# Block 1's gate branch: 512-column products into two banks a slab, the bank pairs in another order, the last GELU behind two tanh groups

## The chip, the cores and the metric

The kernel runs on one core of one Trainium2 chip. The metric is the device time of one execution in microseconds (us), the median of several runs; less is better.

## What is computed

A sequence of 256 positions with 1024 features passes through two transformer-like blocks. The change lies in the first block, in the branch that gates the recurrent unit. Cut to that part, the reference is:

```python
h = rmsnorm(x, norm1_g[l])
u = jnp.einsum('bsd,de->bse', h, w_in[l])
x_rnn, g_rnn, q, k, v, g_br = jnp.split(u, list(cuts), axis=-1)
xa = causal_dwconv(x_rnn, conv_w[l], conv_b[l])
ya = rg_lru(xa, w_r[l], b_r[l], w_i[l], b_i[l], lru_lambda[l]) * jax.nn.gelu(g_rnn)
q = rmsnorm(q.reshape(bsz, s, N_HEADS, HEAD_DIM), q_norm_g[l]).transpose(0, 2, 1, 3)
...
```

`g_rnn` has 1024 features. It is a product of `h` (256 positions, 1024 features) with 1024 columns of `w_in`, and `gelu(g_rnn)` is multiplied into the output of the recurrent unit. Everything is float32 at the interface.

## The kernel before, in words

Each float32 operand of a product is split into a high part (rounded to the format that TensorE multiplies) and a low part (what the rounding left). A product then is three products: high weight by high activation, high weight by low activation, low weight by high activation.

**Slabs.** All weights come in slabs of 128 partitions by 2048 numbers, numbered in the order of use (`s` in the code), through a ring of three buffers. For each slab SyncE loads `raw`, ScalarE (ACT) makes `whi` (line 547), VectorE (DVE) makes `wlo` from `raw` and `whi` (line 1012) and counts `lo_ready`, and TensorE waits for that count before the slab's first matmul. The calls `pre(s)` stand in the programs of ACT and of DVE between their other work, in an order written by hand; each engine runs its program strictly in that order, and semaphores tie the engines together. I call ACT's half of slab s "high part s" and DVE's half "low part s".

**The slabs around the change.** Slabs 0 to 3 are the columns of `x_rnn` (the first two come with the input). Slabs 4 to 7 (`S_G` on) are the gate branch `g_rnn`, 256 features each, and the change is about them. Slab 8 (`S_RI`) holds the small block matrices of the recurrent unit's two gates: eight groups of six matmuls, each group into one PSUM bank, banks 0 to 3 taken twice; ACT empties each by two tanh instructions (line 710), and groups 4 to 7 wait until the bank's earlier group was emptied. Slabs 9 on (`S_Q`) are halves of strips of q, k and v.

**A gate slab before.** `feature_tiles` makes it: for each of 8 slices k and each of 2 tiles of 128 features it calls `three` (lines 1632, 1635, 1636), three matmuls of 256 columns into one half of one PSUM bank, 48 matmuls a slab. DVE multiplies the bank by the position's norm factor `rstd_bc` straight into `gg` (`normed`, line 1056), and ACT takes the GELU of it in place (line 702). Beside that DVE runs the three further taps of the convolution (`taps`, line 1153), ACT makes the high part of `xa` (line 680) and GpSimd (POOL) its low part (line 1568). Behind the last gate slab and low part 9, DVE runs a chain of 23 tiny instructions for softplus (lines 1180 to 1191, "the softplus chain") and only then low part 10.

**PSUM.** The eight banks of 512 columns are also seen as four pairs, `pp[0]` to `pp[3]`. Bank 7, half of `pp[3]`, holds for a while the norm factors turned into a column (`PSB`), which DVE copies into `rstd_half` and `rstd_sq` (lines 1173, 1174) and then counts `rstd2_ready`.

**The other form of product.** `feature_pairs` (lines 1674 and 1676) is in use already for the w_out slabs and the feed-forward layers. High and low activation lie side by side in `ahilo`, so one matmul of 512 columns does both products with the high weight, into a whole bank, and one of 256 columns does the third. A slab then fills two banks, and the half of each bank that holds high weight by low activation must be added to the other. In the feed-forward layers ACT copies that half out (`cross`, line 817), DVE adds the other half to it (line 1335) and then multiplies by `rstd_bc` (lines 1348 and 1368).

The lines of DVE's program around the change:

```python
taps(S_G - 1)
for s in range(S_G, S_RI):
    i = s - S_G
    normed(GROUP_OF[(s, 0)], gg[:, 2 * i:2 * i + 2, :])
    if i == 0:
        e.wait_ge(row_T, 1)
        ...
    if s == S_G + 1:
        pre(s + 3)
pre(S_RI + 1)
```

Of the kernel before, what the change touches and what calls it, by code (L numbers as in the profile page):

```python
# [17 lines left out]
SEQ = 256  # L18
# [140 lines left out]
    return groups  # L159


GROUPS = group_plan()
GROUP_OF = {(s, i): g for g, (s, i, _) in enumerate(GROUPS)}


def bank_plan():


    banks, last, before = [], {}, []
    for g, (s, i, _) in enumerate(GROUPS):  # L170
        if half_strip(s) is not None:
            banks.append(i)
            before.append(None if half_strip(s) else last[i])
            last[i] = g
            continue
        if strip_of(s) is not None:
            b = None
        elif s < S_RI:
            b = s % 4
        elif s == S_RI:  # L180
            b = i % 4
        elif s in (S2_OSWA + 1, S2_OMLA + 1):
            b = 2 + i
        elif out_slab(s) is not None:
            b = ((3, 1) if s < FFN1 else (1, 3))[out_slab(s) % 2]
        elif s in (S2_UQ + 1, S2_UKV):
            b = (3, 2)[i] if s < S2_UKV else (0, 1, 3, 2)[i]
        else:
            b = g % 2
        before.append(last.get(b))  # L190
        banks.append(b)
        last[b] = g
    return banks, before
# [56 lines left out]
def program(nc, t):  # L250
    f32, f32r = mybir.dt.float32, mybir.dt.float32r
    ALU, ACT, AX = mybir.AluOpType, mybir.ActivationFunctionType, mybir.AxisListType.X
    with ExitStack() as ctx:
# [3 lines left out]
        def sem(name):  # L257
            return ctx.enter_context(nc.semaphore(name))
# [103 lines left out]
        def out_pair(s):  # L362

            return pp[((1, 0) if s < FFN1 else (0, 1))[out_slab(s) % 2]]
# [44 lines left out]
            "h_hi", "h_lo", "sq_ready", "ssum", "rms_root", "rstd_ready", "rms_root2", "rstd2_ready"))  # L409
        sq_fold = sem("sq_fold")  # L410
        xa_ready, xa_hi, xa_lo = sem("xa_ready"), sem("xa_hi"), sem("xa_lo")
        g_ready = sem("g_ready")
        t_ready, sqt_ready, ya_ready, ya_hi, ya_lo = (
            sem(n) for n in ("t_ready", "sqt_ready", "ya_ready", "ya_hi", "ya_lo"))
        head_sq, head_sums = sem("head_squares"), sem("head_sums")
# [117 lines left out]
        def _(e):  # L533
# [15 lines left out]
            def pre(s):  # L549
                if s < SLABS:  # L550
                    hi(s % RING, raw_value(s), used_value(s - RING) if s >= RING else None)

            def free_bank(ins):
                ins.then_inc(bank_free["act"], 1)
# [122 lines left out]
            def xa_parts(s):  # L677

                e.wait_ge(xa_ready, s + 1)
                e.activation(pairs[1][0][:, 2 * s:2 * s + 2, :], xa[:, 2 * s:2 * s + 2, :], ACT.Copy).then_inc(xa_hi, 1)  # L680

            for s in range(S_XR, S_G):
# [10 lines left out]
                if s < S_XR + 2:  # L693
                    pre(s + 5)
            pre(S_RI)
            xa_parts(S_G - 1)
            for s in range(S_G, S_RI):
                if s == S_G + 2:
                    pre(s + 3)
                i = s - S_G  # L700
                e.wait_ge(bank_free["dve"], s + 1)
                e.activation(gg[:, 2 * i:2 * i + 2, :], gg[:, 2 * i:2 * i + 2, :], ACT.Gelu_apprx_tanh).then_inc(g_ready, 1)

            for i in range(8):
                g = GROUP_OF[(S_RI, i)]
                e.wait_ge(group_done, g + 1)
                for m in range(2):
                    blk = 2 * (i % 4) + m
                    dst = (T0 if i < 4 else T1)[:, blk, :]
                    ins = e.activation(dst, ps[BANK[g]][:, SEQ * m:SEQ * m + SEQ], ACT.Tanh, scale=0.5,  # L710
                                       bias=halfb[:, 8 * (i // 4) + blk:8 * (i // 4) + blk + 1])
                free_bank(ins)
                if i == 3:
                    pre(S_RI + 2)
            e.wait_ge(bank_free["act"], 8)
# [285 lines left out]
        def _(e):  # L1001
# [13 lines left out]
            def pre(s):  # L1015
                if s < SLABS:
                    lo(s, s % RING)
# [142 lines left out]
            for s in range(S_XR, S_G):  # L1160
                if s >= 2:
                    e.wait_ge(xa_ready, s - 1)
                normed(GROUP_OF[(s, 0)], xrp[:, s % 2, :, KW - 1:])
                if s:
                    taps(s - 1)
                pre(s + 4)
            taps(S_G - 1)
            for s in range(S_G, S_RI):
                i = s - S_G
                normed(GROUP_OF[(s, 0)], gg[:, 2 * i:2 * i + 2, :])  # L1170
                if i == 0:
                    e.wait_ge(row_T, 1)
                    e.tensor_scalar(rstd_half[:, :], PSB[:, 0:2], 0.5, None, ALU.mult)
                    e.tensor_copy(rstd_sq[:, :], PSB[:, 0:2]).then_inc(rstd2_ready, 1)
                if s == S_G + 1:
                    pre(s + 3)
            pre(S_RI + 1)
# [451 lines left out]
        def _(e):  # L1629
# [8 lines left out]
            def bank_ready(g):  # L1638

                s, i = GROUPS[g][:2]  # L1640
                if s in (S2_GA, S2_GA + 1):
                    e.wait_ge(bank_free["dve"], emptied(GROUP_OF[(FFN1, 2 * STEPS - 1)])[1])
                elif s == S2_UQ + 1:
                    e.wait_ge(*((aTe, pair(3)) if i else (cq_lo, 5)))
                elif s == S2_OSWA + 1:
                    e.wait_ge(rope_q_act, 2)
                    e.wait_ge(rope_q_dve, 2)
                elif BEFORE[g] is not None:
                    who, n = emptied(BEFORE[g])
                    e.wait_ge(bank_free[who], n)  # L1650
# [263 lines left out]
            def slab(s, act, layout="feature", ready=always, hook=None):  # L1914

                if s > 2:
                    e.wait_ge(lo_ready, s + 1)
                slot = s % RING
                kind = PLAN[s][1]
                if half_strip(s) is not None:  # L1920
                    half_strips(s, act, ready, hook)
                    return
                if kind == "strip":
                    strips(s, act, lambda k: (hook() if hook and k % 4 == 2 else None, ready(k)))
                    return
                n = sum(1 for x in GROUPS if x[0] == s)
                for i in range(n):
                    g = GROUP_OF[(s, i)]
                    bank_ready(g)
                    out = ps[BANK[g]]  # L1930

                    def at(k, i=i):

                        if (i, k) == (0, 0):
                            pairs_first(s)
                        if (i, k) == ((0, 4) if n == 1 else (n // 2, 0)):
                            pairs_second(s)
                        if (s, i, k) == (S2_OMLA + 1, 1, 0):
                            merge_turn(2)
                        if hook and (i, k) == (0, 4):  # L1940
                            hook()
                        if s == 2 and k % 4 == 0:
                            e.wait_ge(*((lo_ready, 3) if k else (first_lo, KD - 1)))
                        ready(k)

                    if kind == "blocks":
                        for m in range(2):
                            blk = 2 * (i % 4) + m
                            c = 1024 * (i // 4) + P * blk
                            ins = three(out[:, SEQ * m:SEQ * m + SEQ], tuple(w[slot][:, c:c + P] for w in (whi, wlo)),  # L1950
                                        (act[0][:, blk, :], act[1][:, blk, :]), m == 0, True)
                    elif out_slab(s) is not None:
                        ins = feature_pairs(out_pair(s), slot, at, ACT0)
                    elif layout == "feature" and kind == "cols":
                        ins = feature_tiles(out, slot, KD, WIDE, act, [(0, 0), (P, SEQ)], ready=at)
                    elif S2_OSWA <= s < S2_OUT:
                        ins = positions(out, slot, 4, 512, act, slice(0, 512), [(i, 0)],
                                        k0=4 if s >= S2_OMLA else 0, ready=at)
                    elif kind == "nope" or (kind == "kv" and i < 2):
                        ins = feature_tiles(out, slot, 3 if kind == "nope" else 2, HEADS * NOPE, act,  # L1960
                                            [(2 * P * i, 0), (2 * P * i + P, SEQ)], k0=0 if kind == "nope" else 3,
                                            ready=at)
                    elif kind == "rope":
                        ins = positions(out, slot, 3, HEADS * ROPE, act, slice(0, HEADS * ROPE), [(i, 0)], ready=at)
                    else:
                        ins = positions(out, slot, 2, HEADS * VD, act, slice(0, HEADS * VD), [(i - 2, 0)], k0=3,
                                        ready=at, w0=2)
                    ins.then_inc(group_done, 1)
# [263 lines left out]
```

## Time and profile before

| what | value |
|---|---|
| median of 3 runs | 791.01 us (790.78 to 791.04) |
| the profiled execution's own time | 790.45 us |
| its span from first to last instruction | 788.7 us |
| TensorE busy | 781.8 us, 99% |
| VectorE busy | 592.8 us, 75% |
| ScalarE busy | 453.0 us, 57% |
| GpSimd busy | 44.3 us, 6% |
| granted TensorE clock | 0.999 of full speed |

The profile lists for each engine its instructions by start and duration, in us from the start of the span. Two neighbours on one engine overlap a little, so I take the distance of two starts as what an instruction costs its engine. A row's bracket says how long the engine sat idle before it, and what ended that. A matmul's end is modelled; its start is what to read. A row may merge neighbours of one kind, and then gives their number.

### The profile page before, as it was taken

The page shows a single profiled execution, that of the slowest core. Times are in us where ns is not written, and L with a number is a line of the kernel's source. Part 1 is how long each engine was busy: PE and PEld are TensorE (multiplying, and loading weights), DVE is VectorE, ACT ScalarE, POOL GpSimd, SP SyncE. Part 2 cuts the span into 40 slices and gives each one's busy share as a digit, 9 for nine tenths or more (in the row PEclk, how much of TensorE's full clock was granted, in tenths as well). Part 3 has the DMA queues.
Part 4 walks back from the last instruction along what each step waited for, and adds up shares of the span by engine and source line. Part 5 has one row for each costly group of instructions (what it writes and reads, how often), then busy time and mean ns, then how long its engine had stood idle before and what let it go on. Part 6 is the DMA issues. An engine that isn't in the chain of part 4 may idle for free.

```text
span 788.7 us, 11267 instructions
## 1 busy us (share of the span) xinstructions
PE 781.8 (99%) x4246; PEld 669.7 (85%) x4246; DVE 592.8 (75%) x731; ACT 453.0 (57%) x595; POOL 44.3 (6%) x63
## 2 busy tenths in 40 slices
PE   9999999999999999999999999999999999999997
PEld 9998888888888888888888897888788888888886
DVE  6986897666578998778887867787789666666664
ACT  7679765666345654444445758766455545454444
POOL 0220331000000000000000031120000000000000
PEclk9999999999999999999999999999999999999999
DMA  8745555443545455555554452444435545454521
GB/s 331 244 175 193 198 180 214 156 160 128 192 160 207 152 206 184 188 200 197 183 189 160 157 222 89 153 180 160 159 138 212 214 160 208 166 210 167 206 106 53
DMA packets 22100, 141.08 MB, mean 179 GB/s; under 512 B 3410, under 2 KB 3762, under 8 KB 6066
## 3 DMA queue, kind: packets, MB, share of 16 engines
q1 hardware_dynamic: 21682, 140.13, 49.2%
q10 hardware_dynamic: 384, 0.49, 0.2%
q8 instruction: 22, 0.36, 0.2%
q14 instruction: 12, 0.10, 0.0%
HBM read 139.33 MB, written 1.05 MB: 178 GB/s over the span
## 4 chain that ended last, share of the span: by engine, by line
PE 97%; ACT 1%; issue 1%; DVE 1%; ACTq 0%
PE pp L1674 24%; PE pp L1632 18%; PE pp L1636 18%; PE pp L1635 18%; PE pp L1676 12%; PE pp L1818 1%; PE pp L1843 1%; PE pp L1830 1%; PE pp L1994 1%; PE pp L1986 0%; PE pp L1983 0%; PE pp L1979 0%; PE pp L1884 0%; PE pp L1728 0%; PE pp L1756 0%
## 5 line engine op out<-in xcount | busy, mean ns | idle before, releaser
L1012 DVE TENSOR_TENSOR wlo<-raw,whi 128x2048 fp32r<-128x2048 f32 x129 | 296.3, 2298 | 82.5 <-ACT whi L547 81.9
L547 ACT ACTIVATE whi<-raw 128x2048 fp32r<-128x2048 f32 x129 | 246.2, 1910 | 96.9 <-PE pp L1636 81.1
L1674 PE MATMUL pp<-ahilo,whi 128*128 128x512 f32 x832 | 261.9, 396 | 0.1
L1676 PEld LDWEIGHTS pp<-ahilo,wlo 128*128 128x128 f32 x832 | 156.3, 188 | 36.7
L1676 PE MATMUL pp<-ahilo,wlo 128*128 128x256 f32 x832 | 163.5, 278 | 0.0
L1632 PE MATMUL pp<-whi,ahilo 128*128 128x512 f32 (+1 forms) x336 | 133.8, 398 | 0.2 <-ACT first L778 0.2
L1636 PE MATMUL pp<-whi,ahilo 128*128 128x512 f32 (+1 forms) x336 | 130.5, 388 | 0.0
L1635 PE MATMUL pp<-wlo,ahilo 128*128 128x512 f32 (+1 forms) x336 | 130.4, 388 | 0.0
L1674 PEld LDWEIGHTS pp<-ahilo,whi 128*128 128x128 f32 x832 | 128.3, 189 | 2.0 <-DVE wlo L1012 0.3
L817 ACT ACTIVATE qk<-pp 128x512 f32<-128x512 f32 x44 | 26.3, 599 | 118.6 <-PE pp L1676 118.6
L1632 PE MATMUL pp<-whi,ahi 128*128 128x512 f32 (+1 forms) x218 | 85.0, 390 | 0.0
L1635 PE MATMUL pp<-wlo,ahi 128*128 128x512 f32 (+1 forms) x218 | 84.4, 387 | 0.0
L1636 PE MATMUL pp<-whi,alo 128*128 128x512 f32 (+1 forms) x218 | 84.2, 386 | 0.0
L1632 PEld LDWEIGHTS pp<-whi,ahilo 128*128 128x128 f32 x336 | 63.1, 188 | 13.4 <-issue 1.0
L1636 PEld LDWEIGHTS pp<-whi,ahilo 128*128 128x128 f32 x336 | 63.1, 188 | 13.1
L1635 PEld LDWEIGHTS pp<-wlo,ahilo 128*128 128x128 f32 x336 | 63.2, 188 | 11.6
L1335 DVE TENSOR_TENSOR qk<-pp,qk 128x512 f32<-128x512 f32 x44 | 30.3, 689 | 36.9 <-ACT qk L817 36.9
L1636 PEld LDWEIGHTS pp<-whi,alo 128*128 128x128 f32 x218 | 40.9, 188 | 8.4
L1632 PEld LDWEIGHTS pp<-whi,ahi 128*128 128x128 f32 x218 | 41.0, 188 | 7.6 <-issue 0.2
L1635 PEld LDWEIGHTS pp<-wlo,ahi 128*128 128x128 f32 x218 | 41.0, 188 | 7.3
L1632 PE MATMUL pp<-ahilo,whi 128*128 128x256 f32 x96 | 27.5, 286 | 0.0
L1635 PE MATMUL pp<-ahilo,whi 128*128 128x256 f32 x96 | 27.2, 283 | 0.0
(255 smaller groups left out, 826.8 us busy)
## 6 DMA issues: line engine op xcount, KB each, us to landing
raw<-in_slabs SPq DMA_DIRECT2D x125, 1024.0 KB, 4.8
raw<-in_slabs SPq DMA_DIRECT2D x2, 832.0 KB, 4.3
first<-in_first SPq DMA_DIRECT2D x2, 768.0 KB, 7.5
first<-in_first SPq DMA_DIRECT2D x3, 384.0 KB, 4.7
raw<-in_slabs SPq DMA_DIRECT2D x2, 512.0 KB, 9.8
raw<-in_slabs SPq DMA_DIRECT2D x1, 768.0 KB, 4.1
out<-gg SPq DMA_DIRECT2D x3, 256.0 KB, 2.1
xa<-in_final_norm_g SPq DMA_DIRECT2D x1, 512.0 KB, 6.5
```

The lines of the kernel that those rows point to most:

```text
L547: e.activation(whi[slot][:, :], raw[slot][:, :], ACT.Copy).then_inc(hi_ready, 1)
L817: e.activation(dst, banks[:, :, SEQ:2 * SEQ], ACT.Copy).then_inc(f_cross, 1)
L1012: e.tensor_tensor(wlo[slot][:, :], raw[slot][:, :], whi[slot][:, :].bitcast(f32), ALU.subtract).then_inc(lo_ready, 1)
L1335: return e.tensor_tensor(dst, banks[:, :, 0:SEQ], dst, ALU.add)
L1632: e.matmul(out, lhs[0], rhs[0], start=first, stop=False, skip_group_check=True)
L1635: e.matmul(out, lhs[0], rhs[1], start=False, stop=False, skip_group_check=True)
L1636: return e.matmul(out, lhs[1], rhs[0], start=False, stop=last, skip_group_check=True)
L1674: e.matmul(out[:, m, :], w[m][0], act[:, k, :], start=k == 0, stop=False, skip_group_check=True)
L1676: ins = e.matmul(out[:, m, 0:SEQ], w[m][1], act[:, k, 0:SEQ], start=False, stop=k == KD - 1, skip_group_check=True)
L1818: ins = e.matmul(PSS2[:, i, cols], q[:, mine], k[:, keys], start=True, stop=True)
L1830: ins = e.transpose(PSPT2[:, o:o + P], soft[p % 2][:, i, P * j:P * j + P], ident[:, :])
L1843: ins = e.matmul(PSPV2[64 * i:64 * i + 64, mine], v, pT[:, i, keys], start=h == 0, stop=h == 1, skip_group_check=True)
```

## The change

Slabs 4 to 7 are made by `feature_pairs` instead of `feature_tiles`, into the pairs 0, 2, 1, 3. ACT copies the second half of both banks into `gg` (`gate_cross`), DVE adds the first half to it, which frees the bank, and multiplies by `rstd_bc` in a second instruction; ACT's GELU (`branch_gelu`) waits for that. The first two crosses stand on ACT in front of the high part of `xa`'s last quarter, the third behind high part 9, the fourth behind the third GELU; the fourth GELU stands behind two of the eight tanh groups. DVE reads bank 7 (`rstd_half`, `rstd_sq`) before the last taps instead of behind the first gate slab, and TensorE waits for that before slab 7.

```diff
+G_PAIR = (0, 2, 1, 3)
...
+        if S_G <= s < S_RI:
+            b = 2 * G_PAIR[s - S_G]
+            banks.append(b)
+            before.append(last.get(b + 1))
+            last[b] = last[b + 1] = g
+            continue
...
+            def gate_cross(i):
+
+                e.wait_ge(group_done, GROUP_OF[(S_G + i, 0)] + 1)
+                e.activation(gg[:, 2 * i:2 * i + 2, :], pp[G_PAIR[i]][:, :, SEQ:2 * SEQ], ACT.Copy).then_inc(g_cross, 1)
+
+            def branch_gelu(i):
+
+                e.wait_ge(g_scaled, i + 1)
+                e.activation(gg[:, 2 * i:2 * i + 2, :], gg[:, 2 * i:2 * i + 2, :], ACT.Gelu_apprx_tanh).then_inc(g_ready, 1)
+
+            gate_cross(0)
+            gate_cross(1)
             xa_parts(S_G - 1)
             for s in range(S_G, S_RI):
                 if s == S_G + 2:
                     pre(s + 3)
                 i = s - S_G
-                e.wait_ge(bank_free["dve"], s + 1)
-                e.activation(gg[:, 2 * i:2 * i + 2, :], gg[:, 2 * i:2 * i + 2, :], ACT.Gelu_apprx_tanh).then_inc(g_ready, 1)
+                if i > 1:
+                    gate_cross(i)
+                if i < 3:
+                    branch_gelu(i)
...
                 free_bank(ins)
+                if i == 1:
+                    branch_gelu(3)
                 if i == 3:
                     pre(S_RI + 2)
...
+            e.wait_ge(row_T, 1)
+            e.tensor_scalar(rstd_half[:, :], PSB[:, 0:2], 0.5, None, ALU.mult)
+            e.tensor_copy(rstd_sq[:, :], PSB[:, 0:2]).then_inc(rstd2_ready, 1)
             taps(S_G - 1)
             for s in range(S_G, S_RI):
                 i = s - S_G
-                normed(GROUP_OF[(s, 0)], gg[:, 2 * i:2 * i + 2, :])
-                if i == 0:
-                    e.wait_ge(row_T, 1)
-                    e.tensor_scalar(rstd_half[:, :], PSB[:, 0:2], 0.5, None, ALU.mult)
-                    e.tensor_copy(rstd_sq[:, :], PSB[:, 0:2]).then_inc(rstd2_ready, 1)
+                halves, dst = pp[G_PAIR[i]], gg[:, 2 * i:2 * i + 2, :]
+                e.wait_ge(g_cross, i + 1)
+                e.tensor_tensor(dst, halves[:, :, 0:SEQ], dst, ALU.add).then_inc(bank_free["dve"], 1)
+                e.wait_ge(bank_free["dve"], s + 1)
+                e.tensor_tensor(dst, dst, bc2(rstd_bc[:, :], 2), ALU.mult).then_inc(g_scaled, 1)
                 if s == S_G + 1:
                     pre(s + 3)
             pre(S_RI + 1)
...
+                if s == S_RI - 1:
+                    e.wait_ge(rstd2_ready, 1)
...
+                    elif S_G <= s < S_RI:
+                        ins = feature_pairs(pp[G_PAIR[s - S_G]], slot, at, ACT0)
```

What stands on DVE behind the last taps, up to the softplus chain. Before (`gg` is the gate branch, `pp0` and so on the pair of banks, `wlo2` the low part of the slab in ring buffer 2, here slab 8, and `wlo0` that of slab 9):

```order
L1056 TENSOR_TENSOR gg<-pp0,rstd_bc 128x512 [waits group_done]
L1173 TENSOR_SCALAR rstd_half<-pp3 128x2 [waits rstd_row_T]
L1174 COPY rstd_sq<-pp3 128x2
L1056 TENSOR_TENSOR gg<-pp0,rstd_bc 128x512 [waits group_done]
L1012 TENSOR_TENSOR wlo2<-raw2,whi2 128x2048 [waits hi_ready]
L1056 TENSOR_TENSOR gg<-pp1,rstd_bc 128x512 [waits group_done] x2
L1012 TENSOR_TENSOR wlo0<-raw0,whi0 128x2048 [waits hi_ready]
```

The same place in the changed kernel, whose line numbers are its own (its line 1036 is line 1012 of before):

```order
L1199 TENSOR_TENSOR gg<-pp0,gg 128x512 [waits g_cross]
L1201 TENSOR_TENSOR gg<-gg,rstd_bc 128x512 [waits bank_free_dve]
L1199 TENSOR_TENSOR gg<-pp2,gg 128x512 [waits g_cross]
L1201 TENSOR_TENSOR gg<-gg,rstd_bc 128x512 [waits bank_free_dve]
L1036 TENSOR_TENSOR wlo2<-raw2,whi2 128x2048 [waits hi_ready]
L1199 TENSOR_TENSOR gg<-pp1,gg 128x512 [waits g_cross]
L1201 TENSOR_TENSOR gg<-gg,rstd_bc 128x512 [waits bank_free_dve]
L1199 TENSOR_TENSOR gg<-pp3,gg 128x512 [waits g_cross]
L1201 TENSOR_TENSOR gg<-gg,rstd_bc 128x512 [waits bank_free_dve]
L1036 TENSOR_TENSOR wlo0<-raw0,whi0 128x2048 [waits hi_ready]
```

Four instructions that waited for TensorE alone have become eight; four of them wait for ACT's crosses, and the two small readers of `pp3` have gone in front of the last taps.

What stands on ACT from the high part of `xa`'s last quarter on. Before (`first` is where the tanh results go, `whi0` the high part of slab 9):

```order
L680 ACTIVATE ahi1<-xa 128x512 [waits xa_ready]
L702 ACT_TABLE_LOAD
L702 ACTIVATE gg<-gg 128x512 [waits bank_free_dve] x2
L547 ACTIVATE whi0<-raw0 128x2048 [waits group_done,raw_in0]
L702 ACTIVATE gg<-gg 128x512 [waits bank_free_dve] x2
L710 ACTIVATE first<-pp0,halfb 128x256 [waits group_done]
```

The same place in the changed kernel (line 707 is the cross, 712 the GELU, 732 the tanh, 554 the high part, 687 the high part of `xa`):

```order
L707 ACTIVATE gg<-pp0 128x512 [waits group_done]
L707 ACTIVATE gg<-pp2 128x512 [waits group_done]
L687 ACTIVATE ahi1<-xa 128x512 [waits xa_ready]
L712 ACT_TABLE_LOAD
L712 ACTIVATE gg<-gg 128x512 [waits g_scaled] x2
L554 ACTIVATE whi0<-raw0 128x2048 [waits group_done,raw_in0]
L707 ACTIVATE gg<-pp1 128x512 [waits group_done]
L712 ACTIVATE gg<-gg 128x512 [waits g_scaled]
L707 ACTIVATE gg<-pp3 128x512 [waits group_done]
L732 ACTIVATE first<-pp0,halfb 128x256 [waits group_done]
```

The third cross now stands behind the first two GELUs and high part 9, and the fourth behind the third GELU, which itself waits for DVE; the first tanh comes behind all of them. The fourth GELU, not shown, comes behind the second tanh group.

## Rows read from the trace of the kernel before

**Rows 1.** The page: its head, and the chain that ended last by engine.
```profile
span 788.7 us, 11267 instructions
...
PE 97%; ACT 1%; issue 1%; DVE 1%; ACTq 0%
```

**Rows 2.** Timeline of TensorE: start us, us, engine, line, operation, tiles; slabs 4 to 12.
```profile
30.47 0.28 PE L1635 MATMUL pp<-ahilo,whi 128*128 128x256 f32 x1
...
53.39 0.28 PE L1632 MATMUL pp<-ahi,whi 128*128 128x256 f32 x1
...
59.15 0.40 PE L1632 MATMUL pp<-whi,ahilo 128*128 128x512 f32 x1
...
64.61 0.39 PE L1632 MATMUL pp<-whi,ahilo 128*128 128x512 f32 x1
...
75.50 0.39 PE L1632 MATMUL pp<-whi,ahilo 128*128 128x512 f32 x1
```

**Rows 3.** Timeline of TensorE in the feed-forward layer: eight slices of feature_pairs apart.
```profile
244.27 0.63 PE L1674 MATMUL pp<-ahilo,whi 128*128 128x512 f32 x2
...
249.84 0.40 PE L1674 MATMUL pp<-ahilo,whi 128*128 128x512 f32 x1
```

**Rows 4.** Timeline of DVE, from the last taps to low part 12.
```profile
43.49 3.50 DVE L1153 SCALAR_TENSOR_TENSOR xa<-qk,first,xa 128x256 f32<-128x256 f32 x6
46.91 0.68 DVE L1056 TENSOR_TENSOR gg<-pp,rstd_bc 128x512 f32<-128x512 f32 x1
...
47.65 0.67 DVE L1056 TENSOR_TENSOR gg<-pp,rstd_bc 128x512 f32<-128x512 f32 x1
48.25 2.94 DVE L1012 TENSOR_TENSOR wlo<-raw,whi 128x2048 fp32r<-128x2048 f32 x1
...
53.59 0.69 DVE L1056 TENSOR_TENSOR gg<-pp,rstd_bc 128x512 f32<-128x512 f32 x1 [1.80 <-PE pp L1636]
54.20 2.28 DVE L1012 TENSOR_TENSOR wlo<-raw,whi 128x2048 fp32r<-128x2048 f32 x1
56.39 0.17 DVE L1180 TENSOR_SCALAR sp<-sp 128x8 f32<-128x8 f32 x1
...
60.85 2.29 DVE L1012 TENSOR_TENSOR wlo<-raw,whi 128x2048 fp32r<-128x2048 f32 x1
...
71.80 2.29 DVE L1012 TENSOR_TENSOR wlo<-raw,whi 128x2048 fp32r<-128x2048 f32 x1 [2.27 <-ACT whi L547]
```

**Rows 5.** Timeline of GpSimd: the last two low parts of xa.
```profile
41.88 2.85 POOL L1568 TENSOR_TENSOR alo<-xa,ahi 128x512 fp32r<-128x512 f32 x1 [3.01 <-ACT ahi L680]
47.74 1.30 POOL L1568 TENSOR_TENSOR alo<-xa,ahi 128x512 fp32r<-128x512 f32 x1 [3.01 <-ACT ahi L680]
```

**Rows 6.** Timeline of ACT, from the high part of xa to high part 11.
```profile
47.03 0.63 ACT L680 ACTIVATE ahi<-xa 128x512 fp32r<-128x512 f32 x1 [2.98 <-DVE xa L1153]
47.68 1.28 ACT L702 ACT_TABLE_LOAD   x1
48.97 1.15 ACT L702 ACTIVATE gg<-gg 128x512 f32<-128x512 f32 x2
50.03 1.90 ACT L547 ACTIVATE whi<-raw 128x2048 fp32r<-128x2048 f32 x1
...
54.85 3.01 ACT L710 ACTIVATE first<-pp,halfb 128x256 f32<-128x256 f32 x8
57.70 1.96 ACT L547 ACTIVATE whi<-raw 128x2048 fp32r<-128x2048 f32 x1
...
62.61 1.92 ACT L547 ACTIVATE whi<-raw 128x2048 fp32r<-128x2048 f32 x1
```

**Rows 7.** Timeline of DVE in the feed-forward layer: the add, then the multiplication.
```profile
281.82 0.68 DVE L1335 TENSOR_TENSOR qk<-pp,qk 128x512 f32<-128x512 f32 x1
282.54 0.69 DVE L1368 TENSOR_TENSOR qk<-qk,rstd_bc 128x512 f32<-128x512 f32 x1
```

**Rows 8.** Timeline of ACT in the feed-forward layer: one cross.
```profile
276.25 0.60 ACT L817 ACTIVATE qk<-pp 128x512 f32<-128x512 f32 x1 [0.16 <-PE pp L1676]
```

More of the change, by code:

```diff
@@ L411, in program @@
         xa_ready, xa_hi, xa_lo = sem("xa_ready"), sem("xa_hi"), sem("xa_lo")
-        g_ready = sem("g_ready")
+        g_cross, g_scaled, g_ready = sem("g_cross"), sem("g_scaled"), sem("g_ready")
         t_ready, sqt_ready, ya_ready, ya_hi, ya_lo = (
```

## The prediction

> **What bounds the kernel now.** I read the page first: over a span of 788.7 us the chain that ended last is TensorE for 97% [rows 1]. So only what changes the start times of TensorE's matmuls counts, and an instruction on another engine counts as soon as TensorE waits for its result. Then I read TensorE's timeline. Slab 4's second matmul starts at 30.47, and one every 0.12 us follows; slab 8 starts at 53.39, slab 9 at 59.15, slab 10 at 64.61 [rows 2]. There is no gap: 192 matmuls of 0.12 us are 23.04 us, so the four gate slabs ran from 30.35 to 53.39. A slab's last gate is its low part on DVE. Low part 8 ended at 48.25 + 2.94 = 51.19, 2.2 us ahead of its use; low part 9 at 54.20 + 2.28 = 56.48, 2.7 us ahead; low part 10 at 60.85 + 2.29 = 63.14, 1.5 us ahead; low part 12 at 74.09 [rows 4], 1.4 us ahead of 75.50 [rows 2]. The cover is thin, and DVE had only one idle time in this stretch, 1.80 us before 53.59 [rows 4].
>
> **What TensorE saves.** The feed-forward layer shows the new form: eight slices take 249.84 - 244.27 = 5.57 us [rows 3], against 23.04 / 4 = 5.76 us in the old one [rows 2]. Four slabs save 4 x 0.19 = 0.76 us. The number of columns is the same, so there is no more to get. Slab 8 could start at 30.35 + 4 x 5.57 = 52.63, slab 9 at 58.39, slab 10 at 63.85.
>
> **What DVE and ACT get.** An add costs DVE 282.54 - 281.82 = 0.72 us to the next start [rows 7]; that is the wait for its own result. The multiplication lasts 0.69 [rows 7] and costs about 0.61, the distance from 47.65 to 48.25 of an instruction of its size with no wait behind it [rows 4]. So DVE gets 4 x (0.72 + 0.61) = 5.3 us instead of about 2.6. A cross lasts 0.60 on ACT [rows 8] and costs about 0.5; four are about 2 us. The first two are free: ACT sat idle for 2.98 us before 47.03 [rows 6], and slabs 4 and 5 end by 41.5.
>
> **The chain, step by step.** The two small readers of bank 7 before the taps cost at most 0.13 us. I take nothing: POOL's subtraction of 41.88 ran until 44.73 [rows 5], and the taps beside it took 3.50 us [rows 4], so that their start is held by POOL. The first add starts at 46.91, as the first gate instruction does now [rows 4], the first multiplication at 47.63, the second add at 48.24, the second multiplication could start at 48.96.
>
> Here POOL comes in. Its low part of xa ran at 47.74 for 1.30 us [rows 5]. A gate instruction, reading PSUM and one SBUF operand, ran beside it in 0.67 us, undisturbed; low part 8, reading two SBUF operands, started at 48.25 and took 2.94 us against 2.28 for low part 9 [rows 4]: it stood still until POOL was done at 49.04. The new multiplication reads two SBUF operands as well. The first one (47.63 to 48.32) would hold POOL off; POOL then runs until about 49.5, and the second multiplication runs from about 49.5 to 50.2. Low part 8 starts at 50.1, takes 2.28 and ends at 52.4, 0.2 us ahead of TensorE's 52.63. The bounds of this term: nothing (the second multiplication at 48.96, all that follows 0.55 us earlier) and one whole run of POOL, 1.30 us, which is 0.75 more.
>
> The Trainium skill says the same of this pair of engines (SBUF — State Buffer, "SBUF: two separate sides"): they share a port pair under an exclusive lock, taken by a DVE instruction with two SBUF inputs or by GpSimd, and who comes second blocks. It speaks against the change, since the added multiplication is such an instruction and the one removed was not; by it the term would be what I took, and the trace agrees (2.94 against 2.28 us).
>
> ACT: table load until 48.97 [rows 6], first GELU then; the second waits for the second multiplication, 50.2, and costs 0.53 (half of 50.03 - 48.97 [rows 6]). High part 9 starts at 50.75 and costs about 1.83 (its 1.90 [rows 6] less the 0.07 by which neighbours overlap): 52.6. The third cross runs from there to 53.2. DVE has been free since 52.3 and idles: third add 53.2, multiplication 53.9 to 54.6, third GELU 54.65, fourth cross 55.2 to 55.8, fourth add 55.8, fourth multiplication 56.55, low part 9 at 57.15. That one started at 54.20 before; it is 2.95 us late and ends at 59.43. Two idle times of DVE are new, 0.9 us for the third cross and 1.3 us for the fourth.
>
> The softplus chain behind it takes 60.85 - 56.39 = 4.46 us, and 2.19 pass before it (56.39 - 54.20) [rows 4]. So low part 10 starts at 57.15 + 2.19 + 4.46 = 63.80 and ends at 66.1.
>
> ACT's tanh groups start at 55.7 instead of 54.85 and cost 0.75 each (3.01 / 4 [rows 6]). TensorE's group 4 could start at 52.63 + 2.88 = 55.5 but needs bank 0, emptied at 56.5; with the GELU of 0.55 us behind group 1, groups 6 and 7 wait for banks emptied at 58.6 and 59.3. Slab 8 ends at about 60.05, slab 9 starts then and ends at 65.5 (64.61 - 59.15 = 5.46 [rows 2]). That is 1.66 us behind the free schedule, but it is not last: low part 10 comes at 66.1. High part 10, at 59.3 instead of 57.70 [rows 6], ends at 61.2, hidden under the softplus chain.
>
> **Slab 10 starts at 66.15 instead of 64.61: 1.5 us late.** That is 0.76 saved and 2.3 waited. Nothing gives it back. High part 11 starts at about 64.15 instead of 62.61 [rows 6], so that ACT is as late as TensorE, the cover of slab 12 stays near its 1.4 us, and behind that TensorE bounds the kernel to the end and everything is shifted as a whole. For the profiled execution, 790.45 us, the sum gives 792.0; for the median of the runs shown, 791.01, which lies 0.56 higher, **792.5 us**.
>
> **The rivals.** A measurement of this kernel can tell a difference of about 0.2%, 1.6 us, from none: below 789.4 is faster, above 792.6 slower.
>
> *Forecast, 0.52:* as summed, 791.9 to 793.1 (the estimated handovers, some ten between ACT and DVE, may each be off by 0.03 to 0.06 us).
>
> *The lock costs little, 0.20.* If POOL's subtraction gets in ahead of the first multiplication, or the second one hardly waits, the chain moves up by 0.55 us and slab 10 comes at 65.6: 792.0, between 791.5 and 792.3 with the handovers. For it: what POOL costs DVE has been seen on instructions of other sizes only. The rest of the chain stands, so that TensorE still waits 1.7 us.
>
> *A second late buffer, 0.18.* Low part 8 has 0.2 us of cover. If POOL's run costs its whole 1.30, low part 8 comes at 53.1, TensorE starts slab 8 0.5 us late, and every later step of ACT and DVE moves by the same 0.75: slab 10 at 66.9, 793.3; with slower handovers up to 793.9. Clearly slower. It decides from 0.2 us of further delay on.
>
> *The saving comes through, 0.10.* This is the other side. If DVE were never idle between the last taps and low part 10, its work there would be 4 x 1.33 + 2.2 + 2.2 + 4.46 + 2.29 = 16.5 us from 46.91, 63.4, and low part 10 would be in time for 63.85: 791.01 - 0.76 = 790.25. That needs the third cross by 52.3 and the fourth by 53.6, and banks emptied in time for group 4. High part 9 before the third cross and the third GELU before the fourth speak against it, since each engine runs strictly in order. It decides where the 2.2 us of new idle time vanish.
>
> **How the numbers follow.** Forecast and the two rivals beside it lie on one line of one quantity, the start of slab 10. The range of 790.5 to 793.6 takes in the forecast, the small lock, most of the second late buffer, and leaves 790.25 and what lies outside the list out. Slower by over 0.2%: a bit under half of the forecast (0.24) and all but a little of the second late buffer (0.16), 0.40. Faster by over 0.2% would need a gain of 1.6 us, twice what TensorE can save; I leave 0.05 for what I don't see. Within 0.2%: 0.55.
>
> **What the profile of the changed kernel would show.** Right: slab 8 at 52.6; DVE idle before the third and the fourth add, released by ACT's crosses; the second multiplication longer than 0.69 us beside POOL; TensorE short of work before group 4 of slab 8 and before slab 10, the latter released by DVE's low part at about 66.1; from there a constant shift of 1.5 us. Wrong: slab 10 at 63.9 with no idle time of DVE; or a stall of TensorE before slab 8; or a shift that shrinks or grows after slab 12.

## The result, and the profile after

The changed kernel takes 792.27 us against 790.94 us for the kernel before (medians of 22 runs each, on the same chips). The ratio is 1.0017, with a 95% interval from 1.0011 to 1.0023: 1.3 us slower, just inside the 0.2% that the prediction called undiscernible, although so many runs do tell it from nothing. Forecast were 1.5 us more, 792.5 against 791.01. One single execution in this document, of the kernel "GpSimd short" below, took 968.74 us at a mean granted clock of 0.752; its ratio leaves it out.

The page's head, to be read beside [rows 1]:

```profile
span 790.5 us, 11146 instructions
...
PE 89%; DVE 5%; ACT 3%; issue 1%; DMA 1%; SPq 0%; ACTq 0%
```

The span is 1.8 us longer, with 121 instructions fewer. DVE and ACT now appear with 5% and 3% in the chain that ended last. Followed back from the end, the chain leaves TensorE at slab 10's start and from there runs over DVE and ACT alone, down to 9.7 us.

The waits of TensorE in the whole execution (engine, line, what it waited for: us in total, times, longest):

```profile
PE pp L2025 <- DVE ones L1143: 1.1, 1, 1.1
PE pp L1659 <- ACT first L732: 0.9, 2, 0.5
PE pp L1659 <- DVE wlo L1036: 0.3, 1, 0.3
PE pp L1659 <- ACT first L802: 0.2, 1, 0.2
PE pp L1872 <- ACT pT L640: 0.2, 1, 0.2
```

The first and the last two were there before, too (at lines 1994, 1632 and 1843 of that kernel). The second and the third are new. TensorE's timeline shows where they are, against [rows 2]; in the changed kernel lines 1659, 1662 and 1663 are the old 1632, 1635 and 1636:

```profile
30.67 0.50 PE L1703 MATMUL pp<-ahilo,whi 128*128 128x512 f32 x1
...
53.09 0.28 PE L1659 MATMUL pp<-ahi,whi 128*128 128x256 f32 x1
...
56.66 0.39 PE L1659 MATMUL pp<-ahi,whi 128*128 128x256 f32 x1 [0.53 <-ACT first L732]
...
58.77 0.38 PE L1659 MATMUL pp<-ahi,whi 128*128 128x256 f32 x1 [0.41 <-ACT first L732]
...
60.32 0.39 PE L1659 MATMUL pp<-whi,ahilo 128*128 128x512 f32 x1
...
66.22 0.50 PE L1659 MATMUL pp<-whi,ahilo 128*128 128x512 f32 x1 [0.28 <-DVE wlo L1036]
```

Slab 8 starts at 53.09. Its groups 4 and 6 wait for a bank that ACT's tanh empties. Slab 9 starts at 60.32, and slab 10, at 66.22, waits for DVE's low part 10. The brackets understate the waits, since a matmul's modelled end hides part of a gap. The starts tell it all: slab 8 takes 7.23 us instead of 5.76, slab 9 5.90 instead of 5.46.

DVE's timeline, against [rows 4] (line 1199 is the add, 1201 the multiplication, 1036 a low part):

```profile
47.21 0.68 DVE L1199 TENSOR_TENSOR gg<-pp,gg 128x512 f32<-128x512 f32 x1
47.92 0.69 DVE L1201 TENSOR_TENSOR gg<-gg,rstd_bc 128x512 f32<-128x512 f32 x1
48.53 0.68 DVE L1199 TENSOR_TENSOR gg<-pp,gg 128x512 f32<-128x512 f32 x1
49.25 1.06 DVE L1201 TENSOR_TENSOR gg<-gg,rstd_bc 128x512 f32<-128x512 f32 x1
50.24 2.28 DVE L1036 TENSOR_TENSOR wlo<-raw,whi 128x2048 fp32r<-128x2048 f32 x1
53.30 0.69 DVE L1199 TENSOR_TENSOR gg<-pp,gg 128x512 f32<-128x512 f32 x1 [0.79 <-ACT gg L707]
...
55.91 0.69 DVE L1199 TENSOR_TENSOR gg<-pp,gg 128x512 f32<-128x512 f32 x1 [1.18 <-ACT gg L707]
...
57.24 2.28 DVE L1036 TENSOR_TENSOR wlo<-raw,whi 128x2048 fp32r<-128x2048 f32 x1
...
63.88 4.56 DVE L1036 TENSOR_TENSOR wlo<-raw,whi 128x2048 fp32r<-128x2048 f32 x2
```

The two idle times for the third and the fourth cross are there, 0.79 and 1.18 us. Low part 9 starts at 57.24 instead of 54.20, low part 10 (the first of the two in the last row) at 63.88 instead of 60.85.

GpSimd's row beside it, against [rows 5]:

```profile
48.03 1.74 POOL L1595 TENSOR_TENSOR alo<-xa,ahi 128x512 fp32r<-128x512 f32 x1 [3.00 <-ACT ahi L687]
```

It was issued while the first multiplication ran (until 48.61) and took 1.74 us instead of 1.30; the second multiplication was issued while it ran and took 1.06 instead of 0.69.

ACT's timeline, against [rows 6] (line 707 is a cross, 712 the GELU, 554 a high part, 732 the tanh):

```profile
49.27 0.63 ACT L712 ACTIVATE gg<-gg 128x512 f32<-128x512 f32 x1
50.35 0.64 ACT L712 ACTIVATE gg<-gg 128x512 f32<-128x512 f32 x1 [0.45 <-DVE gg L1201]
50.89 1.90 ACT L554 ACTIVATE whi<-raw 128x2048 fp32r<-128x2048 f32 x1
52.69 0.58 ACT L707 ACTIVATE gg<-pp 128x512 f32<-128x512 f32 x1
54.76 0.63 ACT L712 ACTIVATE gg<-gg 128x512 f32<-128x512 f32 x1 [1.48 <-DVE gg L1201]
55.29 0.58 ACT L707 ACTIVATE gg<-pp 128x512 f32<-128x512 f32 x1
55.77 1.56 ACT L732 ACTIVATE first<-pp,halfb 128x256 f32<-128x256 f32 x4
```

The third cross waits for nobody but its turn, behind the second GELU and high part 9; the fourth comes behind a GELU that stood 1.48 us waiting for DVE.

**A mark for comparing profiles.** The first 30 us are not the same in every profile: slab 3's last matmul starts at 29.51 in the kernel before, at 29.93 in the changed one, and at 30.79 in one experiment. So I compare the distance from slab 3's last matmul to slab 10's first, called D below. It is 64.61 - 29.51 = 35.10 before and 66.22 - 29.93 = 36.29 after: 1.19 us more. Behind slab 10 the spans have 788.7 - 64.61 = 724.1 and 790.5 - 66.22 = 724.3 us left: nothing happens there.

The mark leaves one small difference in. DVE's first gate instruction, the first add (in the kernel before the first multiplication), starts 17.28 us behind slab 3's last matmul in the changed kernel and, apart from the last row of the table below, 17.15 to 17.42 us behind it in the others; what moves it stays open. Where slab 10 waits for work that runs over DVE and ACT, the distance from that instruction to slab 10's first matmul, called F, is the cleaner measure: 64.61 - 46.91 = 17.70 before and 66.22 - 47.21 = 19.01 after, 1.31 us more, close to the 1.33 of the medians.

### The profile page after: what moved, and what is told of

Its sections match the earlier page's. It is cut to its first block, busy times and chain, and to the rows that moved or that the text cites. A ratio compares the mean times of both kernels' runs of the same rounds, so it can differ in the third digit from the quotient of the medians.

```text
span 790.5 us, 11146 instructions
## 1 busy us (share of the span) xinstructions
PE 782.4 (99%) x4182; PEld 666.7 (84%) x4182; DVE 595.1 (75%) x735; ACT 455.6 (58%) x599; POOL 44.8 (6%) x63
## 4 chain that ended last, share of the span: by engine, by line
PE 89%; DVE 5%; ACT 3%; issue 1%; DMA 1%; SPq 0%; ACTq 0%
PE pp L1703 24%; PE pp L1659 16%; PE pp L1663 16%; PE pp L1662 16%; PE pp L1705 12%; DVE wlo L1036 2%; DVE xa L1177 1%; PE pp L1847 1%; DMA first<-in_first 1%; PE pp L1872 1%; PE pp L1859 1%; ACT whi L554 1%; PE pp L1913 0%; PE pp L1757 0%; PE pp L1769 0%
## 5 line engine op out<-in xcount | busy, mean ns | idle before, releaser
L1703 PE MATMUL pp<-ahilo,whi 128*128 128x512 f32 x896 | 282.1, 396 | 0.1
L1705 PEld LDWEIGHTS pp<-ahilo,wlo 128*128 128x128 f32 x896 | 168.3, 188 | 39.6
L1705 PE MATMUL pp<-ahilo,wlo 128*128 128x256 f32 x896 | 176.1, 278 | 0.0
L1703 PEld LDWEIGHTS pp<-ahilo,whi 128*128 128x128 f32 x896 | 138.0, 189 | 2.0 <-DVE wlo L1036 0.3
L567 ACT ACTIVATE ahilo<-first 128x256 fp32r<-128x256 f32 x32 | 14.7, 499 | 13.2 <-DVE first L1314 7.8
L1621 POOL TENSOR_TENSOR first<-qk,ropeA 128x64 f32<-128x64 f32 x2 | 1.6, 801 | 342.6 <-ACT qk L756 342.5
```

Of the source, the lines that this page charges most:

```text
L567: e.activation(h_dst[:, c, :], X[:, c, :], ACT.Copy, scale=gains[:, c:c + 1]).then_inc(h_hi, 1)
L1703: e.matmul(out[:, m, :], w[m][0], act[:, k, :], start=k == 0, stop=False, skip_group_check=True)
L1705: ins = e.matmul(out[:, m, 0:SEQ], w[m][1], act[:, k, 0:SEQ], start=False, stop=k == KD - 1, skip_group_check=True)
```

## The experiments

All are edits of the changed kernel except where said. Each was run 11 times (one of them 5 times) beside the kernel before, whose median was 790.85 to 790.92 us. One interval of a ratio is about 0.0009 to either side, 0.7 us, so D and F, read from one profile each, carry the finer statements. The columns "slab 3's last" to "first add" are start times:

| kernel | median us | ratio, 95% interval | slab 3's last | slab 8 | slab 9 | slab 10 | D | first add | F |
|---|---|---|---|---|---|---|---|---|---|
| before | 790.94 | 1 | 29.51 | 53.39 | 59.15 | 64.61 | 35.10 | 46.91 | 17.70 |
| changed | 792.27 | 1.0017 (1.0011 to 1.0023) | 29.93 | 53.09 | 60.32 | 66.22 | 36.29 | 47.21 | 19.01 |
| third cross earlier | 791.49 | 1.0007 (0.9998 to 1.0016) | 30.79 | 53.95 | 60.43 | 66.37 | 35.58 | 48.21 | 18.16 |
| fourth cross earlier | 791.16 | 1.0003 (0.9994 to 1.0012) | 30.17 | 53.33 | 60.06 | 65.53 | 35.36 | 47.56 | 17.97 |
| both crosses | 790.33 | 0.9992 (0.9983 to 1.0001) | 30.05 | 53.21 | 59.07 | 64.54 | 34.49 | 47.46 | 17.08 |
| both, second run | 790.42 | 0.9996 (0.9987 to 1.0005) | 30.04 | 53.20 | 59.05 | 64.51 | 34.47 | 47.44 | 17.07 |
| split | 792.31 | 1.0018 (1.0009 to 1.0027) | 29.94 | 53.82 | 60.44 | 66.38 | 36.44 | 47.35 | 19.03 |
| both and split | 790.92 | 1.0000 (0.9991 to 1.0009) | 29.95 | 53.83 | 59.59 | 65.06 | 35.11 | 47.36 | 17.70 |
| GpSimd short | 791.81 | 1.0012 (1.0002 to 1.0021) | 30.15 | 53.31 | 60.22 | 66.13 | 35.98 | 47.49 | 18.64 |
| GELU later | 792.32 | 1.0018 (1.0009 to 1.0027) | 29.97 | 53.13 | 59.57 | 66.13 | 36.16 | 47.12 | 19.01 |
| short series | 791.78 | 1.0013 (1.0004 to 1.0022) | 29.77 | 52.93 | 60.29 | 65.76 | 35.99 | 47.18 | 18.58 |
| short series, GELU later | 791.67 | 1.0011 (1.0002 to 1.0020) | 29.97 | 53.13 | 59.83 | 65.32 | 35.35 | 47.39 | 17.93 |
| pairs in order | 794.31 | 1.0038 (1.0025 to 1.0052) | 29.95 | 57.27 | 63.01 | 68.48 | 38.53 | 48.81 | 19.67 |

**Is it the order of ACT?** My theory was the serial chain through the third and the fourth cross; the rivals were DVE's added work as such, or the port shared with GpSimd. The third cross alone moved:

```diff
                 i = s - S_G
-                if i > 1:
-                    gate_cross(i)
+                if i == 1:
+                    gate_cross(2)
+                if i == 3:
+                    gate_cross(3)
                 if i < 3:
                     branch_gelu(i)
```

> ACT's third cross moves from behind high part 9 to between the first two GELUs; all else is the changed kernel. My theory (a serial chain of third cross, add, multiplication, third GELU, fourth cross, add, multiplication, low part 9, softplus chain, low part 10 sets slab 10's start): the third add starts behind low part 8 at about 52.5 instead of 53.3, its idle time of 0.79 us vanishes, low part 10 and slab 10 come 0.8 us earlier; 0.8 us less than the changed kernel, ratio to the kernel before about 1.0007. Rival (the softplus chain or the banks of slab 8 hold TensorE whatever ACT's order): no change beyond 0.1 us. Rival (the port lock is what costs): no change, since the second multiplication still runs beside POOL.

The fourth cross alone moved:

```diff
-                if i > 1:
-                    gate_cross(i)
+                if i == 2:
+                    gate_cross(2)
+                    gate_cross(3)
                 if i < 3:
                     branch_gelu(i)
```

> ACT's fourth cross moves from behind the third GELU to in front of it; all else is the changed kernel. My theory: the fourth add follows the third multiplication at about 54.6 instead of waiting until 55.9, so that low part 9 starts 1.2 us earlier; slab 10 is then held by the banks of slab 8 rather than by low part 10, and comes about 1.0 us earlier; ratio to the kernel before about 1.0005. Rival (the softplus chain or the banks hold TensorE whatever ACT's order): no change beyond 0.1 us.

Both moved:

```diff
-                if i > 1:
-                    gate_cross(i)
+                if i == 1:
+                    gate_cross(2)
+                if i == 2:
+                    gate_cross(3)
                 if i < 3:
                     branch_gelu(i)
```

> Both moves at once: third cross between the first two GELUs, fourth cross in front of the third GELU. My theory: DVE is not idle any more between the last taps and low part 10, TensorE waits neither for a bank of slab 8 nor for a low part, and the 0.76 us that the wide products save come through; slab 10 starts at about 63.9 to 64.3 and the kernel takes 0.7 us less than the one before, ratio 0.9991, 2.0 us less than the changed kernel. Rival (DVE's added work alone fills the stretch): low part 10 still comes late, and the ratio stays above 1.0005.

D fell by 0.71, 0.93 and 1.80 us and F by 0.85, 1.04 and 1.93, where 0.8, 1.0 and 2.0 were expected, and the ratios are 1.0007, 1.0003 and 0.9992, where 1.0007, 1.0005 and 0.9991 were. DVE's timeline with both moved:

```profile
50.49 2.28 DVE L1038 TENSOR_TENSOR wlo<-raw,whi 128x2048 fp32r<-128x2048 f32 x1
52.69 0.68 DVE L1201 TENSOR_TENSOR gg<-pp,gg 128x512 f32<-128x512 f32 x1
53.41 0.69 DVE L1203 TENSOR_TENSOR gg<-gg,rstd_bc 128x512 f32<-128x512 f32 x1
54.04 0.69 DVE L1201 TENSOR_TENSOR gg<-pp,gg 128x512 f32<-128x512 f32 x1
54.76 0.69 DVE L1203 TENSOR_TENSOR gg<-gg,rstd_bc 128x512 f32<-128x512 f32 x1
55.37 2.28 DVE L1038 TENSOR_TENSOR wlo<-raw,whi 128x2048 fp32r<-128x2048 f32 x1
62.03 2.29 DVE L1038 TENSOR_TENSOR wlo<-raw,whi 128x2048 fp32r<-128x2048 f32 x1
```

No bracket is left: DVE is not idle once between the first add and low part 10, with the same instructions as in the changed kernel. Its added work alone fits, and so does the longer second multiplication, which is still there (1.07 us). Low part 10 ends at 64.32, 0.2 us ahead of slab 10 at 64.54, and no row of TensorE has a bracket in this stretch. That the loss comes from ACT's order is shown: the four crosses, adds and multiplications are all still made. Since the gain over the kernel before lay at the edge of its interval, the same kernel was run once more:

> The kernel with both crosses moved once more, in a run of its own, because its gain over the kernel before (0.6 us) lay at the edge of the interval. My theory: TensorE's 0.76 us come through, ratio 0.9990 to 0.9994. Rival: no gain, 1.0000.

It gave 0.9996, and the same D within 0.02 us. By the time alone a gain is not proved (both intervals hold 1); both profiles have slab 10 0.6 us earlier than before by D and by F, and both medians are 0.4 to 0.6 us lower. It is the best version found.

**Are the wide products worth anything?** The changed kernel, and the one with both crosses moved, with each wide matmul issued as two. The edit is made in a copy of `feature_pairs` that only the four gate slabs use; what differs from the original is:

```diff
                     for m in range(2):
-                        e.matmul(out[:, m, :], w[m][0], act[:, k, :], start=k == 0, stop=False, skip_group_check=True)
+                        for c in (0, SEQ):
+                            e.matmul(out[:, m, c:c + SEQ], w[m][0], act[:, k, c:c + SEQ], start=k == 0 and c == 0,
+                                     stop=False, skip_group_check=True)
```

> The changed kernel with each 512-column matmul of the four gate slabs issued as two of 256 columns into the same two halves of the bank: 48 matmuls a slab as before the change, with the changed kernel's banks, crosses, adds and multiplications. My theory: TensorE's 0.76 us are lost again, but slab 10 is held by low part 10, and that by ACT and DVE: the time stays within 0.2 us of the changed kernel, ratio to the kernel before 1.0017. Rival (TensorE's own work adds to the waits): 0.76 us more than the changed kernel, ratio 1.0027.

> Both crosses moved, and each 512-column matmul of the gate slabs issued as two of 256. My theory: with the crosses moved TensorE is held by nothing here but its own work, so the narrow matmuls cost their whole 0.76 us: ratio to the kernel before 1.0001 (the kernel with both crosses moved gave 0.9992). Rival (what both moves brought is not TensorE's saving but something else in the new order): the ratio stays at 0.9992.

In the changed kernel the narrow matmuls start slab 8 0.72 us later by the mark, and D changes by 0.15 and F by 0.02 only: the time stays (1.0018). With both crosses moved they cost 0.6 us, D 35.11 against 34.49, and bring the kernel back to 1.0000. So the wide products save 0.6 us where TensorE is the bound, and in the change as it was made they saved next to nothing. The size expected, 0.76 us, was 0.72 for the four slabs; another 0.1 us is lost in slab 8, which takes 5.86 us instead of 5.76 with both crosses moved. TensorE's rows show where, at the first matmul of group 6:

```profile
57.52 0.38 PE L1661 MATMUL pp<-ahi,whi 128*128 128x256 f32 x1
57.74 0.28 PE L1664 MATMUL pp<-alo,whi 128*128 128x256 f32 x1
```

The two starts are 0.22 us apart instead of 0.12, as behind the bank waits of the changed kernel (58.77 to 58.99). Group 6 needs the bank that the third tanh group empties, and that one stands behind the fourth GELU. Its second tanh starts at 56.97 and takes about 0.49 us, so that the bank is free at about 57.45, just as the group is due (57.53). With the matmuls split, the third tanh group starts 0.4 us later, at 56.99, but group 6 is due 0.6 us later, and no such step is seen. That the bank is the cause is read from these times, not tested.

**The port shared with GpSimd.** GpSimd's last low part of xa is cut to 16 columns of 256 in each tile; the rest of it stays zero, which leaves out that correction:

```diff
             for s in range(S_XR, S_G):
                 e.wait_ge(xa_hi, s + 1)
-                e.tensor_tensor(pairs[1][1][:, 2 * s:2 * s + 2, :], xa[:, 2 * s:2 * s + 2, :],
-                                pairs[1][0][:, 2 * s:2 * s + 2, :].bitcast(f32), ALU.subtract).then_inc(xa_lo, 1)
+                n = SEQ if s < S_G - 1 else 16
+                if s == 1:
+                    e.memset(pairs[1][1][:, 6:8, 16:].bitcast(f32), 0.0)
+                e.tensor_tensor(pairs[1][1][:, 2 * s:2 * s + 2, 0:n], xa[:, 2 * s:2 * s + 2, 0:n],
+                                pairs[1][0][:, 2 * s:2 * s + 2, 0:n].bitcast(f32), ALU.subtract).then_inc(xa_lo, 1)
```

> The changed kernel, with GpSimd's last low part of xa cut to 16 of 256 columns of each of its two tiles; the rest of that low part is left at zero (a memset beside the second low part of xa), so that its output differs a little. My theory (a DVE instruction with two SBUF operands stands still while GpSimd's runs): the second multiplication takes 0.69 us instead of 1.06, and since it stands in the chain, slab 10 starts 0.4 us earlier: ratio about 1.0012. Rival (the second multiplication is slower for another reason): it still takes 1.06 us, and nothing moves.

DVE's second multiplication in this kernel:

```profile
49.53 0.69 DVE L1201 TENSOR_TENSOR gg<-gg,rstd_bc 128x512 f32<-128x512 f32 x1
```

It takes 0.69 us, D falls by 0.31 us and F by 0.37. The 0.37 us by which it was longer came from GpSimd, and it lay on the path. Both instructions read two SBUF operands.

**Banks of slab 8 and the softplus chain.** The fourth GELU behind four tanh groups:

```diff
-                if i == 1:
-                    branch_gelu(3)
                 if i == 3:
+                    branch_gelu(3)
                     pre(S_RI + 2)
```

> The changed kernel with the fourth GELU behind four tanh groups instead of two. My theory: TensorE's wait before group 6 of slab 8 (0.41 us) vanishes, but low part 10 does not move, so slab 10 starts at the same time: ratio 1.0017. Rival (the waits for banks add to the end): 0.4 us less, 1.0012.

The softplus series with three terms, which is less exact:

```diff
-            for odd in (13, 11, 9, 7, 5, 3, 1):
+            for odd in (5, 3, 1):
```

> The changed kernel with the softplus series cut from seven terms to three, eight tiny DVE instructions and 1.6 us less (the series is less exact). My theory: low part 10 comes 1.6 us earlier, but then the end of slab 9, late by the banks of slab 8, holds slab 10: it starts 0.4 to 0.5 us earlier, not 1.6; ratio 1.0012. Rival (low part 10 is the only limit): 1.3 us or more earlier, ratio below 1.0003.

Both together:

> The changed kernel with both edits that were tried apart: the softplus series cut to three terms (less exact), and the fourth GELU behind four tanh groups. Alone the first gave about 0.4 us and the second nothing. My theory (slab 10 takes the later of low part 10 and the end of slab 9, which the banks of slab 8 hold back): together they give about 0.8 us, since the bank wait of 0.41 us now lies on the path: ratio 1.0007. Rival (each stands alone): 0.4 us, ratio 1.0012.

The GELU alone moved slab 9 by 0.79 us (by the mark), D by 0.13 and F not at all; TensorE's wait has moved, as its row before slab 10 shows, 0.90 us instead of 0.28:

```profile
66.13 0.50 PE L1658 MATMUL pp<-whi,ahilo 128*128 128x512 f32 x1 [0.90 <-DVE wlo L1035]
```

The series alone took 1.62 us out of DVE's chain (low part 10 starts 5.02 us behind low part 9, 62.23 - 57.21, instead of 6.64), but only 0.30 us out of D and 0.43 out of F, where 0.4 to 0.5 were expected: slab 9, late by the banks, is next. Together they gave 0.94 us at slab 10 by D and 1.08 by F, more than the 0.8 expected, but the ratio came out at 1.0011, not 1.0007. The expectation had stopped at slab 10. Three slabs on, TensorE waits again, for ACT's emptying of q's first strip:

```profile
82.09 0.47 PE L1658 MATMUL pp<-whi,ahilo 128*128 128x512 f32 x1 [0.28 <-ACT qk L755]
```

Behind slab 10 724.6 us are left, 0.3 more than in the changed kernel. ACT's high part 11 starts at 64.22, no earlier than in the changed kernel (64.20), because the cut was on DVE, and from there ACT runs without an idle time up to that emptying. So ACT's own delay against [rows 6], 1.6 us or 1.15 by the mark, stands and is, as I read it, the third limit in a row; no experiment took it away.

**A stall before the chain.** The order of the pairs:

```diff
-G_PAIR = (0, 2, 1, 3)
+G_PAIR = (0, 1, 2, 3)
```

> The changed kernel with the pairs of banks taken in the order 0, 1, 2, 3. Slab 5 then writes banks 2 and 3 and must wait until DVE has emptied slab 3's bank, at about 38.3 us, so TensorE stands still for some 2.2 us before slab 5. My theory: that stall is nearly all hidden, since low part 10 holds slab 10 anyway and the two bank waits in slab 8 vanish: slab 10 0.2 to 0.3 us later, ratio 1.0020. Rival (a stall of TensorE counts wherever it is): 2.2 us more than the changed kernel, ratio 1.0045.

This was the worst miss: 794.31 us, ratio 1.0038, where 1.0020 was expected and 1.0045 by the rival. TensorE waits 2.36 us before slab 5, near the 2.2 computed. But slab 8 starts 4.2 us later than in the changed kernel. TensorE's stretches of this kernel follow: stretch and length, the busy times of PE, PEld, DVE, ACT and POOL, then the granted clock, the busy share of the DMA engines and GB/s:

```profile
38.80:40.10 1.30, 1.19 (x6) 1.09 (x7) 1.30 (x3) 1.30 (x3) 0.50 (x1) 1.00 0.60 101
40.10:43.50 3.40, 3.40 (x12) 2.94 (x12) 3.22 (x5) 2.12 (x2) 1.20 (x1) 0.50 0.64 270
43.50:47.00 3.50, 3.50 (x21) 3.04 (x20) 3.50 (x9) 0.62 (x1) 1.67 (x1) 1.00 0.50 154
```

TensorE worked again from 38.91. Some 1.2 us later the granted clock fell to half (1.2 of 2.4 GHz) and stayed there for 3.4 us. At half the clock that is an estimated 1.7 us more, and the rows bear it out: 4.16 us by the mark less the stall of 2.36 are 1.8. And high part 8 on ACT, which stands ahead of the first two crosses, waits for slab 5:

```profile
46.38 1.93 ACT L554 ACTIVATE whi<-raw 128x2048 fp32r<-128x2048 f32 x1 [4.15 <-PE pp L1705]
```

So the first add started at 48.81 instead of 47.21, slab 7 ended behind the turn of the fourth cross, and both moved the chain. Of 4.2 us about half was hidden (slab 10 is 2.2 us later by the mark), but not nearly all. One of the five executions took only 792.79 us, at a mean granted clock of 0.998 against 0.996 to 0.997 for the other four (794.19 to 794.45). It has no profile, so whether the half clock was shorter or missing there stays open; it is close to the 1.0020 that was expected without one.

## Why the prediction was right

- **TensorE's saving.** Slab 8 was forecast for 52.63 and started at 53.09, with slab 3's end 0.42 us later in this execution: right to 0.04 us (0.72 us saved, 0.76 forecast).
- **The two small readers of bank 7.** Taken at nothing, and it was: the first add came 17.28 us behind slab 3's last matmul, the first gate instruction before 17.40.
- **The lock.** The term was taken as 0.54 us (49.5 - 48.96) and measured 0.37 (1.06 against 0.69), between the forecast and the rival with the small lock. GpSimd's run was sized nearly right: it ended at 49.77, 0.52 us behind the second multiplication's start at 49.25. What was wrong was to charge the whole of that rest: the multiplication grew by 0.15 us less. The kernel before shows the same, [rows 4] and [rows 5]: low part 8 started 0.79 us before GpSimd was done (49.04) and grew by 0.66. The short run of GpSimd shows the cause and the price, 0.31 us of D and 0.37 of F. The Trainium skill's rule of an exclusive lock (SBUF — State Buffer, "SBUF: two separate sides") holds in both directions here: GpSimd's instruction grew by 0.44 us behind the first multiplication, and the second one grew behind GpSimd's, by 0.15 us less than the rest of its run.
- **The chain over ACT.** Forecast idle times of DVE 0.9 and 1.3 us, measured 0.79 and 1.18. Moving the crosses removed them one by one and together; this was the step on which the forecast rested, and it is shown.
- **The banks of slab 8.** Forecast were waits before groups 4, 6 and 7; those before 4 and 6 are there, 0.53 and 0.41 us, and none shows before group 7. Slab 9 was forecast for 60.05 and came at 60.32, the same to 0.15 us with the late start. It was right that they are not last: the GELU moved behind four tanh groups left F at 19.01. They stand close behind, though, 0.43 us by the short series.
- **Slab 10.** Forecast 1.54 us late; by the mark 1.19, by F 1.31, by the times 1.33. Counted from the first add, the sum was 0.23 us too large (19.24 against 19.01), and about 0.17 of that is the lock's size.
- **Nothing gives it back.** Right: 724.1 and 724.3 us behind slab 10.
- **The rivals.** The second late buffer did not occur: low part 8 ended at 52.52, 0.6 us ahead of slab 8, because in this execution TensorE's start was later by 0.42 us and DVE's by 0.30 only, and the lock was smaller. The saving that comes through did not occur, and the experiment with both crosses moved shows that its condition was named rightly (the third cross by 52.3, the fourth by 53.6, and no idle time on DVE): there it did come through, with 0.6 us instead of 0.76. Its sum of 16.5 us for DVE's work left the lock out: 64.32 - 47.46 = 16.86 were measured, about the lock's 0.37 more, and that just fitted.

## What to carry to other kernels

A faster form of an instruction on the bounding engine is worth what is left when its helpers' added steps are put into the other engines' strict orders: here 0.7 us of saving on TensorE was outweighed by two copies placed behind work that they did not depend on. Write down for each added step the earliest time at which its input is there and the time of its turn; where they differ and someone waits for the result, move the step before looking for anything else. And when a limit is removed, ask which one is next, then which one is next after that: three stood within 1 us of each other here, on DVE's low part 10, on the banks of slab 8, and on ACT three slabs later.

## What was not expected of the hardware

In the profile with the pairs in order, a stall of TensorE of 2.36 us was followed by 3.4 us at the half clock, from 40.10 to 43.50, which cost about 1.7 us beyond the stall. The changed kernel's stalls of 0.5 us and less show no such thing: the granted clock is 1.00 in its stretches from 53.00 to 70.00. No experiment separated the stall from what else this kernel does there, so that the one brought the other is likely, not shown. A wait that seems to be covered later can cost more than its length.
